# Decimated scan of a state-space layer: two pairs' products alternate between parts of the TensorE array, and every engine's order in the first stage is written out anew

## The reference: what is computed

```python
def fox_s5_mixer(x, w_in, f_bias, a_re, a_im, log_dt, b_re, b_im, c_re, c_im, d_skip, w_glu, b_glu, w_out):
    z = x @ w_in
    q, k, v, f_logit, u = jnp.split(z, [...], axis=-1)
    att = forgetting_attention(q.reshape(shp), k.reshape(shp), v.reshape(shp), f_logit + f_bias)
    y = s5_scan(u.reshape(B, S, S5_GROUPS, S5_GROUP), a_re, a_im, log_dt, b_re, b_im, c_re, c_im, d_skip)
    y = jax.nn.gelu(y.reshape(B, S, S5_WIDTH))
    y = y * jax.nn.sigmoid(y @ w_glu + b_glu)
    return jnp.concatenate([att, y], axis=-1) @ w_out
...
    # s5_scan: h[t] = lb * h[t-1] + bu[t], complex, one lb per group and state
    _, _, h_re, h_im = lax.associative_scan(combine, (a_re_t, a_im_t, bu_re, bu_im), axis=1)
    y = jnp.einsum('bsgp,gcp->bsgc', h_re, c_re) - jnp.einsum('bsgp,gcp->bsgc', h_im, c_im)
    return y + d_skip * u
```

## Time and profile before

| | |
|---|---|
| median of 3 runs | 1931.15 us (1929.08 to 1931.25) |
| the profiled execution | 1924.49 us, its span 1922.8 us |
| PE busy | 1786.7 us, 93% of the span |
| DVE, ACT, POOL busy | 526.8, 376.2, 171.6 us |
| fox, from pair 0's input product to the first output product | 44.5 us to 147.4 us of the span |

### The profile page before, as it was taken

One profiled execution on the slowest core, in us unless ns is written; L12 is line 12 of the kernel. 1 busy time (PEld: TensorE's weight loads), 2 busy tenths in 40 slices (PEclk: granted clock), 3 DMA queues, 4 the chain that ended last, 5 costly groups with the idle time before them and its releaser, 6 DMA issues.

```text
span 1922.8 us, 22232 instructions
## 1 busy us (share of the span) xinstructions
PE 1786.7 (93%) x7308; PEld 938.2 (49%) x7309; DVE 526.8 (27%) x1226; ACT 376.2 (20%) x690; POOL 171.6 (9%) x376
## 2 busy tenths in 40 slices
PE   7999899899989989999999999999999988898886
PEld 6654333676633338766765485444443333233232
DVE  7552300787540031431472130011140000000002
ACT  3252311222231121041241000111041111110101
POOL 0220122000012200000000000000011110110100
PEclk9989999899979989999999999999999999999999
DMA  9005499575319974324313343422458999999995
GB/s 378 24 1 219 170 416 422 208 287 232 147 71 410 422 304 175 132 104 169 143 44 132 153 156 150 156 111 95 175 199 336 423 422 422 421 422 422 422 422 237
DMA packets 70731, 468.88 MB, mean 244 GB/s; under 512 B 7880, under 2 KB 12656, under 8 KB 15360
## 3 DMA queue, kind: packets, MB, share of 16 engines
q1 hardware_dynamic: 66304, 457.56, 58.7%
q10 hardware_dynamic: 4352, 10.35, 1.5%
HBM read 466.82 MB, written 1.06 MB: 243 GB/s over the span
## 4 chain that ended last, share of the span: by engine, by line
PE 73%; DMA 17%; DVE 5%; ACT 1%; issue 1%; SPq 0%; POOL 0%; ACTq 0%; DVEq 0%; POOLq 0%
PE bank L255 18%; DMA ring_sb<-stream 17%; PE bank L268 14%; PE bank L2820 10%; PE bank L1782 4%; PE bank L2863 4%; PE bank L2830 4%; PE bank L2757 2%; PE bank L301 2%; PE bank L1006 1%; PE bank L2060 1%; PE bank L589 1%; PE bank L996 1%; PE bank L1417 1%; PE bank L607 1%
## 5 line engine op out<-in xcount | busy, mean ns | idle before, releaser
L2820 PE MATMUL bank<-ring_sb,scratch_sb 128*64 128x512 f32 x1536 | 345.8, 597 | 56.0 <-DMA ring_sb<-stream 49.8
L268 PE MATMUL bank<-xT_sb,ring_sb 128*128 128x256 f32 x1216 | 264.5, 379 | 0.0
L2820 PEld LDWEIGHTS bank<-ring_sb,scratch_sb 128*64 128x64 f32 x1536 | 115.0, 137 | 282.0 <-issue 273.1
L268 PEld LDWEIGHTS bank<-xT_sb,ring_sb 128*128 128x128 f32 x1216 | 230.6, 190 | 33.6 <-issue 2.5
L255 PE MATMUL bank<-ring_sb,xT_sb 128*128 128x512 f32 x416 | 179.4, 592 | 0.0
L255 PE MATMUL bank<-ring_sb,scratch_sb 128*128 128x512 f32 x384 | 167.7, 598 | 7.3 <-ACTq L2424 3.9
L2863 PE MATMUL bank<-ring_sb,scratch_sb 128*64 128x512 f32 x768 | 171.9, 596 | 0.0
L2981 DVE TENSOR_TENSOR scratch_sb<-scratch_sb,bank 128x256 f32<-128x256 f32 (+1 forms) x32 | 17.8, 555 | 406.9 <-PE bank L2820 279.8
L255 PEld LDWEIGHTS bank<-ring_sb,xT_sb 128*128 128x128 f32 x416 | 78.9, 190 | 97.7 <-issue 97.3
L2830 PE MATMUL bank<-scratch_sb 128*128 128x512 f32 x256 | 123.7, 606 | 0.0
L3097 ACT ACTIVATE scratch_sb<-bank 128x256 f32<-128x256 f32 (+1 forms) x96 | 47.1, 491 | 380.7 <-PE bank L2845 204.2
(11 more groups left out here) (414 smaller groups left out, 1621.0 us busy)
## 6 DMA issues: line engine op xcount, KB each, us to landing
ring_sb<-stream SPq DMA_DIRECT2D x432, 1024.0 KB, 10.7
rows_sb<-rows ACTq DMA_DIRECT2D x12, 512.0 KB, 4.7
xT_sb<-xT SPq DMA_DIRECT2D x2, 512.0 KB, 7.3
x_sb<-x SPq DMA_DIRECT2D x1, 1024.0 KB, 20.3
scratch_sb<-bias_by_distance ACTq DMA_DIRECT2D x1, 1024.0 KB, 5.3
out<-x_sb ACTq DMA_DIRECT2D x2, 512.0 KB, 2.6
scratch_sb<-decay ACTq DMA_DIRECT2D x1, 768.0 KB, 5.4
small_sb<-small SPq DMA_DIRECT2D x1, 640.0 KB, 10.9
```

What stands on the lines that cost most here:

```text
L268: mm = pe.matmul(t[:, m * SEQ:(m + 1) * SEQ], w[:, k % 4, n0:n0 + P], actT[:, k, :], start=k == 0, stop=k == kt - 1)
L2820: mm = pe.matmul(t[e * TILE:(e + 1) * TILE, :], self.xs[e][:, kk, :], ws[e][:, k, :], start=kk == 0, stop=kk == KT - 1, skip_group_check=True)
```

## The change

Three things. `pair_inputs` issues the input products of two pairs in alternation: the two pairs differ in m, so neighbours in the stream stand in different 32-row parts of the array and write to different banks. `pair_sums` does two pairs at once: first four `fold` products that alternate between two column groups, then four `K0` products, now alternating as well. And the orders of PE, ACT and DVE from the value product to the last head are new: PE's and ACT's as plain lists, DVE's with `turn_in` of both pairs of a couple ahead of the first's scan and with `HEADS_BEHIND` shifted. `keep_v` is only what ACT did inline before.

```diff
-    HEADS_BEHIND = ((), (0,), (1,), (2,), (3,), (4,), (5,), (6, 7))
+    HEADS_BEHIND = ((), (), (0,), (1,), (2,), (3,), (4, 5), (6, 7))
...
+    def pair_inputs(self, pe, q):
+
+        pairs = (2 * q, 2 * q + 1)
+        banks = [self.net.T.open(pe, ("bu", p), self.INPUT) for p in pairs]
         for odd in range(2):
...
             for part in range(2):
                 at = (2 * odd + part) * self.HALF
...
+                for first, weights in ((True, self.LB), (False, self.B)):
+                    for p, t in zip(pairs, banks):
+                        k, m = self.tile(p, odd)
+                        rows = slice(32 * m, 32 * m + 32)
+                        mm = pe.matmul(t[:, at:at + self.HALF], weights[part][rows, k, :],
+                                       self.uT[rows, k, 0 if first else 1, :], start=first, stop=not first,
+                                       skip_group_check=True)
...
+    def pair_sums(self, pe, q):
+
+        T, pairs = self.net.T, (2 * q, 2 * q + 1)
+        key = ("y", q // 2)
+        t = T.bank[T.jobs[key][0]] if q % 2 else T.open(pe, key, self.SUMS)
+        pe.wait_ge(self.s("turn_kept"), 2 * q + 2)
         for odd in range(2):
...
+            for p in pairs:
+                k, m = self.tile(p, odd)
+                pe.matmul(t[32 * m:32 * m + 32, odd * SEQ:(odd + 1) * SEQ], self.net.fold[:, 0:32],
+                          self.strips[p % 2][:, odd * SEQ:(odd + 1) * SEQ], start=True, stop=False,
+                          skip_group_check=True)
+        for odd in range(2):
+            for p in pairs:
+                k, m = self.tile(p, odd)
+                rows = slice(32 * m, 32 * m + 32)
+                mm = pe.matmul(t[rows, odd * SEQ:odd * SEQ + self.HALF], self.K0[rows, k, :], self.uT[rows, k, 0, :],
+                               start=False, stop=True, skip_group_check=True)
...
+        self.pair_output(pe, 0)
         vs = [net.use_unit(pe) for _ in range(2)]
         t = T.open(pe, ("fox_v", 0), rest)
         net.part(pe, t, vs, net.xT, 0, range(4))
-        self.pair_output(pe, 0)
+        self.pair_output(pe, 1)
+        self.pair_inputs(pe, 2)
+        self.scores(pe, 2)
         T.close(("fox_v", 0), net.part(pe, t, vs, net.xT, 0, range(4, KT)))
-        self.pair_input(pe, 3)
+        self.pair_sums(pe, 0)
+        self.pair_output(pe, 2)
+        self.turn_p(pe, 0)
+        self.scores(pe, 3)
+        self.pair_inputs(pe, 3)
...
+        self.pair_sums(pe, 2)
+        self.pair_output(pe, 6)
+        self.turn_p(pe, 4)
+        self.head_out(pe, 3)
+        self.scores(pe, 7)
+        self.turn_p(pe, 5)
+        self.head_out(pe, 4)
+        self.pair_output(pe, 7)
+        self.turn_p(pe, 6)
+        self.head_out(pe, 5)
+        self.pair_sums(pe, 3)
         self.turn_p(pe, HEADS - 1)
         self.head_out(pe, HEADS - 2)
-        self.pair_sums(pe, 7)
...
         for p in range(8):
-            self.turn_in(dve, p)
+            if p % 2 == 0:
+                self.turn_in(dve, p)
+                self.turn_in(dve, p + 1)
             self.scan(dve, p)
```

More of the change, by code:

```diff
@@ L841, in tiles @@
         return slice(j, j + 5, 4)
[L843 to L845 removed]
+    def pair_inputs(self, pe, q):
+        pairs = (2 * q, 2 * q + 1)
+        banks = [self.net.T.open(pe, ("bu", p), self.INPUT) for p in pairs]
         for odd in range(2):
[L847 to L848 removed]
             for part in range(2):
                 at = (2 * odd + part) * self.HALF
[L851 to L856 removed]
+                for first, weights in ((True, self.LB), (False, self.B)):
[5 more added lines that the diff above has]
+                                       skip_group_check=True)
+                        if (odd, part, first) == (1, 1, False):
+                            self.net.T.close(("bu", p), mm)
     def pair_output(self, pe, p):
@@ L913, in tensor @@
         pe.wait_ge(self.s("u_kept"), 4 + 2)
-        for p in range(2):
-            self.pair_input(pe, p)
+        self.pair_inputs(pe, 0)
         net.product_T(pe, "fox_k", net.xT, banks=rest)
-        self.pair_input(pe, 2)
+        self.pair_inputs(pe, 1)
         pe.wait_ge(self.s("c_ready"), 1)
@@ L1048, in scalar @@
             self.head_exps(act, i)
-            if i:
-                self.head_weigh(act, 0)
-            t = T.take(act, ("fox_v", i))
-            s(act.activation(self.vv[:, i, :], t[:, :], ACT.Copy))
-            T.free(act, ("fox_v", i))
-            act.sem_inc(self.s("qkv_kept"), 1)
-        for p in range(2, 8):
-            for n, h in enumerate(self.HEADS_BEHIND[p]):
-                if h >= 2:
-                    self.head_exps(act, h)
-                    self.head_weigh(act, h - 1)
-                if n == 0:
-                    self.keep_turn(act, p)
-                self.head_turned(act, h - 1)
-                if h >= 2:
-                    self.head_kept(act, h - 2)
-        self.head_weigh(act, HEADS - 1)
-        self.head_turned(act, HEADS - 1)
-        self.head_kept(act, HEADS - 2)
-        self.head_kept(act, HEADS - 1)
+        self.head_weigh(act, 0)
+        self.keep_v(act, 0)
+        self.keep_turn(act, 2)
+        self.head_turned(act, 0)
+        for h in (2, 3):
+            self.head_exps(act, h)
+            self.head_weigh(act, h - 1)
+        self.keep_turn(act, 3)
+        self.head_turned(act, 1)
+        self.keep_v(act, 1)
+        self.head_kept(act, 0)
+        self.keep_turn(act, 4)
+        self.head_exps(act, 4)
+        self.head_weigh(act, 3)
+        self.head_turned(act, 2)
+        self.head_kept(act, 1)
+        self.head_exps(act, 5)
+        self.head_weigh(act, 4)
+        self.keep_turn(act, 5)
+        self.head_turned(act, 3)
+        self.head_kept(act, 2)
+        self.keep_turn(act, 6)
+        self.head_exps(act, 6)
+        self.head_weigh(act, 5)
+        self.head_turned(act, 4)
+        self.head_kept(act, 3)
+        self.head_exps(act, 7)
+        self.head_weigh(act, 6)
+        self.head_turned(act, 5)
+        self.head_kept(act, 4)
+        self.keep_turn(act, 7)
+        self.head_weigh(act, 7)
+        for h in (6, 7):
+            self.head_turned(act, h)
+            self.head_kept(act, h - 1)
+        self.head_kept(act, 7)
         self.after_exps(act)
@@ L1076, in scalar, with keep_v @@
             act.sem_inc(self.s("glu_sig"), 1)
+    def keep_v(self, act, i):
+        t = self.net.T.take(act, ("fox_v", i))
+        self.net.ac(act.activation(self.vv[:, i, :], t[:, :], ACT.Copy))
+        self.net.T.free(act, ("fox_v", i))
+        act.sem_inc(self.s("qkv_kept"), 1)
     def spread(self, act, dense, compact):
@@ L1229, in vector @@
                     self.head_scale(dve, h - 1)
+                if h == 4:
+                    self.y_keep(dve, 0)
         self.head_scale(dve, HEADS - 1)
```

55 lines of the change are left out of this document (15 added, 40 removed).

## The result

The changed kernel takes 1917.01 us (median of 3 runs, 1915.49 to 1918.86) against 1931.15: ratio 0.9931, 95% interval 0.9908 to 0.9953. Timed again, as the experiment `after_again`, it is 0.989 [0.987, 0.991]. It is faster, by 3 us less than was forecast. Of the sum behind the forecast, the terms for the packed products came near, the waits came out smaller, and what was expected of the clock is not seen between the two profiles.

What follows compares the result with a forecast made beforehand. PE's own stream was taken as the bound, busy 98.13 of the stage's 102.90 us. Inputs -6.9, sums -7.5, clock -4.5 and waits +1.7 gave -17.2 us: median 1914 us against 1931.15, range 1907 to 1924.

Steps and rivals of the forecast that it cites:

- Item 1: PE's input products: two pairs in alternating row groups last about as long as one pair, 2.06 us a block; saves 6.9 us.
- Item 2: PE's sums: folds and K0 of two pairs overlap, 1.6 us a block; saves 7.5 us, 1.8 less if K0 run serially.
- Item 3: PE's clock in the stage: the new order gives back half of some 9 us lost at the lower level, 4.5 us.
- Item 4: PE's waits in the stage: the old 4.8 us go, new ones of 6.5 us come; net loss 1.7 us.
- Item 5: DVE scans wait for POOL's turn_back: about 5 us of DVE lost, already counted in the waits of item 4.
- nothing packs: Rival: neither input products nor sums overlap on PE, only the order counts; -7 us, 1924 us; chance 0.08.
- only half packs: Rival: K0 and folds of one bank, or the inputs, do not overlap; -11.5 us, 1919.5 us; chance 0.14.
- DVE becomes the bound: Rival: POOL's 16 products each hold DVE 1.27 us, deciding from about 8 us of waits; -8 us, 1923 us; chance 0.06.
- a drain at each alternation: Rival: each change between PE row groups costs 0.19 us and nothing overlaps; +8 us, 1939 us; chance 0.03.
- The gain is lost again behind the stage: Rival: a later stretch loses the gain, for instance by starting in a colder clock; no change; chance 0.03.
- E: Experiments' theory: PE products that fill few rows of the array, one behind the other, bring the lower clock.
- F: Experiments' rival theory: which PE stretches run at the lower clock is chance, or follows the stage's length, not the order.

Runs made afterwards that it cites:

- orders_only: Changed kernel with its new orders, but input products and sums one pair after the other, nothing alternating: 1936.59 us, ratio 1.0021 to the kernel before.
- inputs_plain: Changed kernel with input products one pair after the other, sums still alternating: 1923.84 us, ratio 0.9957 to the kernel before.
- spread_all: Changed kernel with value product cut and spread between scores and inputs, scores 7 later, ACT's keep_turn(5) and head 6's exponentials earlier, DVE rotations apart: 1907.02 us, ratio 0.9862.
- pack_old_order: Kernel before, in its old order, with the alternating input products and sums of two pairs put in: 1917.37 us, ratio 0.9917.
- tail_order: Changed kernel with scores 7 ahead of the sums of pairs 4 and 5, and ACT's keep_turn(5) and head 6's exponentials earlier: 1911.55 us, ratio 0.9875.
- rotate_apart: Changed kernel with DVE doing each pair's rotation just ahead of its own scan: ratio 0.9883 to the kernel before.
- v_first: Changed kernel with the value product's first part and pair 0's output between scores 0 and scores 1: 1907.83 us, ratio 0.986; run again 1908.59 us, 0.9874.
- scores_in_a_row: Changed kernel with scores 2 directly behind scores 0 and 1, ahead of pair 0's output: ratio 0.988 to the kernel before.

## Why the prediction was right, and where its sum was wrong

The forecast was a stage shorter by 17.2 us, ending at about 130, and 1914 us. The stage became 13.2 shorter and ended at 134.2; the time is 1917.0, inside the range. Work, clock and waits stand apart in the table. The packing, which was to bring most of the gain, is confirmed by `orders_only` and `inputs_plain`; that the median came so near is partly luck, as said below.

*Item 1, input products: -6.9 forecast, -5.5 measured.* The mechanism is right: `inputs_plain` against the changed kernel isolates it, and the block takes 1.98 us where 2.06 were forecast from the earlier trace rows. The 1.4 missing are those that I expected from pairs standing together even without alternation (3.42 instead of twice 1.95, at three places). In `orders_only` they stand so, yet its work is 0.2 us above that of before; so the new order pays about as much elsewhere, and I had counted nothing for that. Where exactly was not taken apart.

*Item 2, sums: -7.5 forecast, -7.7 measured;* the block 1.54 us instead of 1.6. The four `K0` of two row groups, which write to one bank, take 0.55 us, where each alone took 0.33. The rule of the Trainium skill, "TensorEngine Tiling (Array Packing)", Restrictions and Gotchas, that different row tiles cannot access one PSUM bank simultaneously, would have made it some 0.45 us more; as a rule of time the trace doesn't bear it out here, where the two write to different partitions of that bank.

*Item 3, clock: -4.5 forecast, +0.3 measured.* **Between the two profiles, this is the step that failed.** I took half of what the clock costs as given back, because an output block follows the first scores directly and the tail is filled. But 20.5 us ran slow before and 20.5 after, and the signs named for it (mean above 0.93, the value product's first part at 3.7 us) read 0.89 and 5.52. The clock fell at 64.07, among the first scores and before the output block behind them began (68.75), so that block could not keep it up. My bounds of 0 to 9 had no room for a loss at all, and the runs show that there is one to be had: 34.1 us slow with the same order unpacked, 36.1 with half of it, 37.5 with the old order packed. The term should have been 0 with bounds of both signs, some -8 to +8: between `spread_all` and `pack_old_order` lie 34 us of slow time, 14.4 us of stage by the part in which PE was busy.

The pair of profiles is not the last word on this term, though. The profiled execution of before had a mean clock of 0.976, near the top of its 43 timed ones (0.964 to 0.977, mean 0.9729). Against that mean the changed kernel's executions did have more clock, 0.9750 in the three of the result and 0.9775 in `after_again`, the latter worth some 9 us of the whole. How much of it lies in the stage, no run shows: the kernel before has one profile only. And the reason given for the term is not confirmed, since `orders_only`, with the same order, has 0.9710.

*Item 4, waits: 6.5 forecast, 4.2 measured,* so -0.6 where +1.7 was expected. The two large pieces came where and as large as forecast, 2.13 for head 6's weights (2.0) and 1.37 ahead of the sums of pairs 4 and 5 (1.2), and the last sums waited 0.51 (0.7). What did not come were head 0's 0.8 and most of the 1.8 of small pieces. Laying the four lists side by side with durations from the trace found the real waits; `tail_order` then removed 2.0 us of them.

*Item 5, DVE against POOL: right.* A scan beside POOL takes 1.3 us instead of 0.42; scans and additions lose 4.1 + 0.5 us against before, in which 0.8 had been lost already, so 5.4 where 5 were forecast. And it is hidden but for 0.8 us at most (`rotate_apart`); DVE even waits 4.04 us for PE at 110.57. The rule of the Trainium skill, "SBUF — State Buffer", Who interferes with whom, agrees for scans too, by these 1.3 us: the two that started while POOL worked, at 62.36 and 63.69, ended 0.28 us behind the end of POOL's product.

The stage's sum against the forecast: clock 4.8 us worse, work 1.4 worse, waits 2.3 better, together 3.9 of the 4.0 us by which it ended late.

*Behind the stage* the forecast had one for one. The profile shows 4.1 us more there, but two profiles of `v_first` differ by 7.5 there. Less half of the busy time that ran slow, the part behind the stage takes 1750.6 us before, 1752.6 and 1750.8 in the two profiles of the changed kernel, and 1747.9 to 1752.8 over all kernels. So no loss is shown, and one of about 2 us is not excluded. SP's long wait became 11.8 us shorter (103.5 to 91.7), so the weights' stream did move with the stage. The profiled execution came 8.5 us late and the median only 3, since the profiled execution of before, with its high clock, lay 6.7 us below its median and that of the changed kernel 1.5. These 5.2 us are luck, and no merit of the sum.

The rivals: *nothing packs* and *only half packs* are refuted by `orders_only` and `inputs_plain`, *DVE becomes the bound* by the 5.4 us lost, under its 8, and by its wait for PE, *a drain at each alternation* by the 1.98 us of a block. *The gain is lost again behind the stage* is not shown.

**What stays open** is what brings the lower clock. E is supported by `v_first` (13.7 twice) and `spread_all` (3.4), and not by `scores_in_a_row` (17.1 where it wanted 24, and a clock of 0.9795 when timed). F, chance, fits that run, but not the clocks that repeat with the kernel. The sum of slow time repeated for the same order in both pairs of profiles, but no rule that I can state gives 20.5, 34, 36 and 37 for four of the orders. Nor do the medians follow the profiled stages one for one: `spread_all` has a stage shorter by 2.7 us than `v_first`, and the same median: timed, its clock is only 0.002 higher, and multiplied by the clock it takes 1870.2 us against 1869.0, which fits its added work.

## What to carry to other kernels

Where small products use one row or column group of TensorE, writing those of two groups in alternation takes four tenths off their time (1.98 us for 3.42); one place in the old trace where two such streams happen to meet was enough here to forecast the block to 4%. Before a gain by order is added to one by packing, ask what the order is for: here it was worth nothing alone, and with the packing it halved the waits, by one profile each, and those could be forecast by laying the engines' lists side by side. And a change of order came with 3 to 37 us of slow clock here, as much time as the whole packing gains, so that term gets bounds of both signs. Compare kernels at one clock: time multiplied by the mean granted clock of each execution separated here a gain of 12 us at full clock from a scatter of 22 us among executions of the kernel before. Orders worth a trial are those that put a product of all rows between products of few, though the reason for it is not shown.

## What the runs showed of the hardware

- TensorE's clock fell to 0.50 (1.2 of 2.4 GHz) at 64.07 though PE had been busy all of the 19.55 us since 44.52, and stayed there for 10.24 us, all of them busy. In the last 3.55 us ahead of the fall ran input products of 32 rows and scores of 64 and 8, ahead of them 14 us of a product with all 128. Over twelve kernels with the same products the slow part of the stage went from 3.4 to 37.5 us, in one to six pieces.
- The clock explains most of what varies from run to run: behind the stage two profiles of one kernel differ by 7.5 us, of which 7.2 are half of the busy time that ran slow.
- Four `K0` of 32 rows by 32 columns, from two row groups into one bank, each to its own 32 partitions, ran side by side: 0.55 us for the four, 0.33 for one alone.
- A scan of 128x128 with its operands in SBUF took 1.3 us beside a product of POOL and 0.42 without; POOL lost little, 1.42 and 1.31 us instead of 1.27 where its product met a scan already running.
- `spread_all`, which cuts the value product into more parts among other shapes, has 1.7 us more work of PE in the stage; that the cuts are the cause was not tested alone.
